# Two transformer blocks on one core: rotation and gates moved into the input projection, chunks run ahead, value products spread

## The reference

```python
def token_mixer(h, w_in, ...):
    proj = h @ w_in
    qk_ml, v_ml, o_ml, gates, q_at, kv_at = jnp.split(proj, cuts, axis=-1)
    qk_ml = jax.nn.silu(causal_dwconv(qk_ml, ml_conv_w, ml_conv_b))
    ...
    i_pre = gates[..., :ML_H] + ml_i_b
    logf = jax.nn.log_sigmoid(gates[..., ML_H:] + ml_f_b)
    h_ml = mlstm_chunkwise(q_ml, k_ml, v_ml, i_pre, logf)
    h_ml = rms_norm(h_ml, ml_norm_g) * jax.nn.sigmoid(o_ml)
    q_at, k_at = rope(q_at, pos), rope(k_at, pos)
    o_at = rms_norm(sliding_window_attention(q_at, k_at, v_at, attn_sinks), attn_norm_g)
    return jnp.concatenate([h_ml, o_at], axis=-1) @ w_out

# mlstm_chunkwise, one chunk (m_t is the running maximum, b the cumulated logf)
sqk = einsum('bhtd,bhsd->bhts', qc, kc) * exp(dmat - m_t[..., None])
num = einsum('bhts,bhsd->bhtd', sqk, vc) + w_inter[..., None] * einsum('bhvk,bhtk->bhtv', C, qc)
den = sum(sqk, -1) + w_inter * einsum('bhk,bhtk->bht', n, qc)
h = num / maximum(abs(den), exp(-m_t))[..., None]
C_new = decay[..., None, None] * C + einsum('bhsv,bhsk->bhvk', vc * ws[..., None], kc)
```

## Time and profile before

| | us |
|---|---|
| median of the runs (2887.23 to 2889.32) | 2887.88 |
| profiled execution | 2889.09 |
| its span, from first to last instruction | 2887.3 |
| TensorE busy | 2528.2 (88%) |
| VectorE busy | 1344.2 (47%) |
| ScalarE busy | 866.9 (30%) |
| mean granted TensorE clock | 0.936 of full |

### The profile page before, as it was taken

One profiled execution on the slowest core, in us unless ns is written; L12 is line 12 of the kernel. 1 busy time (PEld: TensorE's weight loads), 2 busy tenths in 40 slices (PEclk: granted clock), 3 DMA queues, 4 the chain that ended last, 5 costly groups with the idle time before them and its releaser, 6 DMA issues. The chain is left out here.

```text
span 2887.3 us, 29375 instructions
## 1 busy us (share of the span) xinstructions
PE 2528.2 (88%) x11143; PEld 2026.2 (70%) x11143; DVE 1344.2 (47%) x1509; ACT 866.9 (30%) x1185; POOL 283.4 (10%) x212
## 2 busy tenths in 40 slices
PE   4899867365979999999999895888889999999998
PEld 2688666253857888888887582666668888888887
DVE  3554256565255455444445515888452333323333
ACT  2321223165343222222223324777332111111111
POOL 0000000044100000000001230545110000000000
PEclk8899966677989999999999897999899999999999
DMA  6246200200221111111112210000211111111111
GB/s 211 86 139 221 75 0 0 88 0 0 102 88 37 51 44 58 44 51 44 45 50 102 84 52 15 1 0 0 88 44 44 44 49 52 44 51 48 47 51 66
DMA packets 163843, 167.09 MB, mean 58 GB/s; under 512 B 7025, under 2 KB 147137, under 8 KB 162753
## 3 DMA queue, kind: packets, MB, share of 16 engines
q1 hardware_dynamic: 162337, 160.95, 17.2%
q0 software_dynamic: 1440, 5.24, 0.4%
HBM read 144.16 MB, written 22.02 MB: 58 GB/s over the span
## 5 line engine op out<-in xcount | busy, mean ns | idle before, releaser
L263 PE MATMUL ps<-hhi,whi 128*128 128x512 f32 x1984 | 773.5, 390 | 8.2 <-DVE cbuf L779 4.0
L265 PE MATMUL ps<-hhi,wlo 128*128 128x512 f32 x1984 | 772.6, 389 | 0.0
L264 PE MATMUL ps<-hlo,whi 128*128 128x512 f32 x1984 | 772.4, 389 | 0.0
L212 DVE TENSOR_TENSOR wlo<-raw,whi 128x1024 fp32r<-128x1024 f32 x180 | 234.7, 1307 | 523.8 <-ACT whi L207 523.8
L263 PEld LDWEIGHTS ps<-hhi,whi 128*128 128x128 f32 x1984 | 372.9, 188 | 87.6 <-DVE cbuf L779 4.4
L264 PEld LDWEIGHTS ps<-hlo,whi 128*128 128x128 f32 x1984 | 372.9, 188 | 77.4
L265 PEld LDWEIGHTS ps<-hhi,wlo 128*128 128x128 f32 x1984 | 372.7, 188 | 77.4
L207 ACT ACTIVATE whi<-raw 128x1024 fp32r<-128x1024 f32 x180 | 186.4, 1050 | 426.8 <-PE ps L1781 299.9
L1898 DVE TENSOR_TENSOR arena<-arena,ps 128x1024 f32<-128x1024 f32 x176 | 214.8, 1220 | 155.6 <-PE ps L1781 154.5
L1779 PE MATMUL ps<-hid_hi,whi 128*128 128x512 f32 x704 | 275.2, 391 | 0.0
L1780 PE MATMUL ps<-hid_lo,whi 128*128 128x512 f32 x704 | 274.1, 389 | 0.0
(11 more groups left out here) (276 smaller groups left out, 2889.4 us busy)
## 6 DMA issues: line engine op xcount, KB each, us to landing
raw<-in_w_up SPq DMA_DIRECT2D x66, 512.0 KB, 3.7
raw<-in_w_down SPq DMA_DIRECT2D x44, 512.0 KB, 3.4
raw<-in_w_in SPq DMA_DIRECT2D x32, 512.0 KB, 5.5
arena<-in_w_ada SPq DMA_DIRECT2D x32, 512.0 KB, 4.5
x_park<-arena SPq DMA_DIRECT2D x3, 4096.0 KB, 12.5
raw<-in_w_gate SPq DMA_DIRECT2D x22, 512.0 KB, 3.6
cbuf<-in_w_ada SPq DMA_DIRECT2D x16, 512.0 KB, 5.3
raw<-in_w_out SPq DMA_DIRECT2D x16, 512.0 KB, 4.0
```

Source lines behind the costliest of these rows:

```text
L212: nc.vector.tensor_tensor(wlo[:, w.off % RING, :], raw[:, w.off % RAW, :], whi[:, w.off % RING, :].bitcast(F32), ALU.subtract).then_inc(lo ...
L263: nc.tensor.matmul(acc[:, tok], whi[:, s, ws], hhi[:, k, tok], start=(k == 0), stop=False)
L264: nc.tensor.matmul(acc[:, tok], whi[:, s, ws], hlo[:, k, tok], start=False, stop=False)
L265: mm = nc.tensor.matmul(acc[:, tok], wlo[:, s, ws], hhi[:, k, tok], start=False, stop=(k == DK - 1))
```

## The change

In the input projection the tiles get another order: six attention tiles first, then 8 convolution tiles, 4 values, 4 output gates. The gate products come directly behind the pair of the first two tiles. TensorE makes the rotation of tile `ROPED[n]` behind the product of tile n + 2, VectorE does its three operations there, and GpSimd stores the rotated tile. The gate rows are worked out by VectorE and ScalarE in tiles 1 to 5, and three of them are stored in DRAM (`gate_rows`). Blocks `ml_gates` and `rope` are gone. The chunks read keys, queries and values in place, get their three rows by broadcast loads, have two buffers for most things, and turn up to two chunks ahead; the loops over chunks are unrolled. In the second attention the sixteen value matmuls are made in four parts, one in each unit of the next group, into two halves of the accumulator.

```diff
-                return columns(a["w_in"], w + (-T_IN), 8 if o - T_IN >= 16 else 0)
+                r = o - T_IN
+                return columns(a["w_in"], w + (20 if r < 2 else 14 if r < 6 else -6), 8 if r < 6 else 0)
...
+        ROPED = (0, 2, 3, 4, 5)
...
+            @block.sync
+            def _(sp):
+                norm_mix.sp(sp)
+                sp.dma_start(cos_1, a["rope"][:, 0, :]).then_inc(tables_in, 16)
+                sp.dma_start(sin_1, a["rope"][:, 1, :]).then_inc(tables_in, 16)
+                for t in range(4, N_IN + 4):
+                    load(sp, At(t), tile_source(At(t)))
+                    for n in late_at(t - 2):
+                        if n == 0:
+                            sp.wait_ge(rope_step, 3 * len(ROPED))
...
+                norm_mix.pe_pair(pe, 0)
+
+                pe.wait_ge(gate_hi, 2)
...
+                def rotate(n):
+                    t = ROPED[n]
+                    pe.wait_ge(raw_copied, t + 1)
+                    if n:
+                        pe.wait_ge(rope_step, 3 * n - 2)
+                    for hf in range(2):
+                        tok = slice(hf * HALF, (hf + 1) * HALF)
+                        mm = nc.tensor.matmul(down[0][:, tok], rotA[:, :], cbuf[:, t % 4, tok], start=True, stop=True)
+                    mm.then_inc(rotated, 1)
+
+                for t in range(2, N_IN):
+                    pe.wait_ge(up_free, t + 1)
+                    product(pe, up[t % 2], At(t))
+                    if 2 <= t <= 6:
+                        rotate(t - 2)
...
+                    if t == 2:
+                        act.wait_ge(g_dve, 4)
+                        nc.scalar.activation(row_a, row_a, ACT.Exp, scale=-1.0).then_inc(g_act, 1)
...
+                def rope(r):
+                    t = ROPED[r]
+                    c = cbuf[:, t % 4, :]
...
+                    dve.wait_ge(rotated, r + 1)
+                    nc.vector.tensor_tensor(turned_sin, down[0][:, :], sin_1, ALU.mult).then_inc(rope_step, 1)
+                    nc.vector.tensor_tensor(c, c, cos_1, ALU.mult).then_inc(rope_step, 1)
+                    dve.wait_ge(rope_step, 3 * r + 2)
+                    nc.vector.tensor_tensor(c, c, turned_sin, ALU.add).then_inc(rope_step, 1)
...
+                for t in range(18, N_IN):
+                    pool.wait_ge(up_free, t + 3)
+                    pool.dma_start(spill[:, t - 18, :], cbuf[:, t % 4, :]).then_inc(spilled[t % 4], 16)
+                pool.wait_ge(rows_stored, 48)
+                for i in range(4):
+                    pool.wait_ge(spilled[i], 16 * (3 if i < 2 else 2))
...
+        with nc.Block("ml_chunks") as block:
...
+                for c in range(NB):
+                    if c >= 2:
+                        sp.wait_ge(c_done, c - 1)
+                    for r, v in enumerate((bc_a, bc_w, bc_m)):
+                        sp.dma_start(v[c % 2], rows_dram[r][:, tok(c)].partition_broadcast(P)).then_inc(rows_in[c % 2], 16)
+                sp.wait_ge(c_turned, NB)
+                sp.dma_start(kvq, spill[:, 4:10, :]).then_inc(kvq_in, 16)
...
+                turn(0)
+                update(0)
+                turn(1)
+                for c in range(NB):
+                    outputs(c)
+                    if c + 2 < NB:
+                        turn(c + 2)
+                    if c + 1 < NB:
+                        update(c + 1)
...
+                def exponents(c):
+                    dve.wait_ge(rows_in[c % 2], 48 * (c // 2 + 1))
+                    if c >= 2:
+                        dve.wait_ge(c_main, c - 1)
+                    nc.vector.tensor_tensor(weights_[c % 2], bc_a[c % 2],
+                                            causal[:, :].unsqueeze(1).to_broadcast([P, ML_H, P]), ALU.add).then_inc(c_arg, 1)
...
+                for c in range(NB):
+                    if c + 1 < NB:
+                        weigh(c + 1)
...
+                    dve.wait_ge(c_den, 3 * c + 3)
+                    dve.wait_ge(c_read, c + 1)
+                    nc.vector.tensor_tensor(hml[:, :, tok(c)], hml[:, :, tok(c)], m, ALU.mult).then_inc(c_done, 1)
+                    if c + 2 < NB:
+                        exponents(c + 2)
...
-            ps_t, ps_o = down[0], down[1][:, 0:512]
+            ps_t = down[0]
+            ps_o = [down[1][:, 0:512], down[1][:, 512:1024] if full else down[1][:, 0:512]]
...
-                            if gr_before(n, e) is not None:
-                                values(gr_before(n, e), ((e - 1) // units) % 2, unit(n, e) + (-1))
+                            if group_under(n, e) is not None:
+                                if full:
+                                    part = e % units
+                                    values(group_under(n, e), 1 - e // units, unit(n, e) + (-1),
+                                           range(2 * part, 2 * part + 2))
...
-        rope_stage("rope", 0, rotA, True, False)
         attention("attn", False, Heads())
```

More of the change, by code:

```diff
@@ L8 @@
+import math
 from contextlib import ExitStack
@@ L696, in block_kernel @@
         qk, vt = ar(0, DK, T), ar(32, ML_H, T)
[L697 to L721, removed]
+        hml = qk[:, 0:ML_H, :]
+        cos_1, sin_1, turned_sin = ar(48, T), ar(52, T), ar(56, T)
         late_row = [ar(48 + 4 * i, D) for i in range(3)]
@@ L745, in late_add @@
[L745 to L823, removed]
@@ new lines, in block_kernel @@
+        value_tok = [heads(ar(68, 512)), heads(gateF[:, :, :].rearrange("p a b -> p (a b)"))]
+        state = heads(cbuf[:, 3, :], 2 * P)
+        ps_num, ps_den, ps_s = heads(up[0][:, 0:512]), up[1][:, 0:512], heads(up[1][:, 512:1024])
+        ps_k, ps_v, ps_u = heads(down[0][:, 0:512]), heads(down[0][:, 512:1024]), down[1]
+        qa = ar(16, 4, T)
+        ka, va = ar(32, T), ar(36, T)
+        kvq = ar(16, 6, T)
+        rows_in = [sem("chunk_rows0"), sem("chunk_rows1")]
+        c_turned, c_tokens, c_arg, c_exp, c_query, c_weights, c_ones = (
+            sem("chunk_" + x) for x in ("turned", "tokens", "exponents", "exps", "queries", "weights", "decays"))
@@ new lines, in block_kernel, with tok, _ @@
+        c_main, c_update, c_read, c_den, c_den_free, c_state, c_zero, c_done, kvq_in = (
+            sem("chunk_" + x) for x in ("outputs", "update", "read", "den", "den_free", "state", "zero", "done", "kvq"))
+        with nc.Block("ml_chunks") as block:
+            def tok(c):
+                return slice(c * P, (c + 1) * P)
+            @block.sync
+            def _(sp):
+                for c in range(NB):
[5 more added lines that the diff above has]
+                sp.dma_start(kvq, spill[:, 4:10, :]).then_inc(kvq_in, 16)
+                sp.wait_ge(kvq_in, 16)
@@ L995, in body @@
-                    for h in range(ML_H):
-                        mm = nc.tensor.matmul(ps_u[:, h * 256:h * 256 + 256], ktok[:, h, :], vw[:, h, :], start=True,
-                                              stop=True)
-                    mm.then_inc(c_upd, 1)
-                    if more:
-                        early(c + 1)
-                        pe.wait_ge(c_den, c.val(2, 2))
-                        pe.wait_ge(c_read, c.val(add=1))
-                        late(c + 1)
-                chunk_loop(pe, ahead, body)
+                    mm.then_inc(c_main, 1)
```

490 lines of the change are left out of this document (304 added, 186 removed).

## The result

The changed kernel takes 2850.14 us (median; 2847.13 to 2854.65) against 2888.6 for the kernel before beside it (2887.23 to 2890.31): a ratio of 0.987, 95% interval 0.9858 to 0.9883. It is faster by 38 us (1.3%) where I had forecast 89, and lies outside my range of 2783 to 2840. The profiled execution took 2854.65 us.

The account below looks back on a forecast made before the run. TensorE was taken to bound the input projection, serial chains the gate, rope and chunk stages, VectorE the second attention. Savings 13.9 + 19.5 + 35.4 + 21 = 89.8 from 2889.1 gave 2799 us, range 2783 to 2840.

Parts of the forecast that it names:

- L: Chunks: time of the three broadcast loads, taken as 5.0 us, exposed on VectorE in chunks 2 to 7 and once at the start.
- Rival A: Chunks: the three broadcast loads don't overlap, each taking 3 to 3.7 us, about 10 together; time 2836; chance 0.20.
- Rival D: Chunks: all reads of one array go through one place in memory; at 20 us a load, time 2904; chance 0.03.
- The estimate of 3.8 us: Chunks: broadcast load time from a fixed 2.0 us plus bytes at 436 GB/s; sum some 8 us lower; not adopted.
- The sum around L: Chunks: start, six periods and end give 127.2 us against 146.7, 19.5 saved; 7 us lost per us more of load.
- the periods: Chunks: six periods of 15.15 us each, made of load, mask to weights, weights, state and scaling.
- the start: Chunks: from block start to the first state update, 20 us (17 to 24).
- the end: Chunks: after state 6 the last outputs end 9 us later, then the last chunk takes 7.3 us.
- Input projection: Gate products moved behind the first pair, rotations added on TensorE; chunks start at 357.3 instead of 371.2, saving 13.9 us.
- Rope stage: Stage before the chunks, dropped whole with the 3 MB reload hidden; 35.4 us saved.
- Second attention: Value matmuls in four parts; a block takes 26.2 us against 29.18, seven blocks save 21 us.
- Rival B: Second attention: parts stand in series with the turn; block 28.2 us, only 7 us saved, time 2813; chance 0.12.

## Why the prediction was wrong

**The step that failed is the size of L**, the time of a chunk's three broadcast loads: taken as 5.0 us, it is 12.3. I had bounded it by 3.5 and 12.6 and taken the value near the slope of larger loads, "nearest to the load of the same run length". That load has another address for each partition. Own addresses gave 4.7, so for such loads the slope was right; what it could not tell was that 128 partitions reading one piece, with all pieces a multiple of 4096 bytes apart, move a quarter as fast. Rival A was right that the loads don't overlap, and too low in price (10, or 10.3 by the 5.3 in its sum). Rival D, reads that meet in one place of the memory, is nearest to what the layouts showed; it had 3 in 100 and was priced only from 17.8 up, so 12.3 fell between the rivals. The estimate of 3.8 us that I made from the Trainium skill (DMA: Bandwidth & Descriptors, Anatomy of one DMA) rests on a fit for DMAs that GpSimd issues; SyncE issues these, and the wait was 12.3. My range reached 2840 and thus left out the upper bound of L that I had myself worked out: 12.6 gives 2799 + 7 x 7.6 = 2852.

**The sum around L held.** "7 us lost for each us more of L" gives 2799 + 7 x 7.3 = 2850 with the measured L, and 2850.14 was measured. That this agrees to 0.2 us is luck: the profiled execution took 2854.65, and the smaller errors below partly cancel. With L at 4.7, the kernel with own addresses took 2797.4. Period minus wait is 9.8 us there (14.5 - 4.7), 9.8 in the changed kernel (22.1 - 12.3) and 9.7 without a wait; I had 10.15. The wait after `c_done` exposes the load wholly, as argued: taking it away removed all of it. The chunks took 179.9 us where I had 127.2: the periods are 6 x 7.0 of that, the start 9 (first state update after 29.3 us instead of 20), the end 1.5.

**Input projection: right.** 13.1 us saved against 13.9. TensorE had no gap up to its last product, which ends at 352.2 (352.4 predicted); the copy, the store at 353.61 and its 2.9 us follow, and the blocks change at 358.1, 1.6 after the landing where I had 0.5.

**Rope stage: right, with a price unseen.** The stage is gone. The 3 MB reload is over before it is needed, but it is issued 0.5 us behind the last chunk's rows and runs beside them: that wait is 13.39 instead of 12.1, and with pieces at 4224 bytes it was 11.58 instead of 6.6. Where the rows load fast it hardly shows (4.92 instead of 4.6 with own addresses). That the reload causes it is read from the times of issue, not tested.

**Second attention: right in kind, 2.8 us too low** (23.8 against 21). Blocks of 25.8 at the full clock are below the 26.2 that I had; where the clock is 0.94 they take 27.3. Rival B (28.2) is out, and with it the fear that the parts stand in series.

**What I had left out:** the stages between lost 5.5 us in the profiled execution. 2.8 of them lie in the long feed-forward part from the norm on (its 769.3 us became 772.1), where TensorE's clock came up at another time after its waits (0.85 and 0.91 between 851.6 and 881 us, where the same stretch before had 1.00). The kernels with own addresses and with a place for each chunk had 770.7 and 769.2 there, so this isn't the change's doing but moves from kernel to kernel. The net is 89.8 - 52.7 - 0.8 + 2.8 - 5.5 + 0.6 (the first attention's start, 11.8 instead of 12.4) = 34.2, and 34.5 was the difference of the spans.

## What to carry over

A double buffer whose next load waits for the last reader of the same buffer hides nothing when that reader runs just ahead of the first user: look at what frees a buffer, not at how many there are, and give loads of data that is ready long before a place of their own. Where the trace has no load of the kind that a change adds, the price belongs near the bounds and the range must hold both of them, the more so when one unknown is multiplied by seven. When all partitions read the same few hundred bytes, store them so that what is read together is one run; twelve neighbouring pieces did as well, and padding by one whole piece nearly so.

## What the hardware showed

- Shared reads in pieces of 512 bytes, all a multiple of 4096 bytes apart, moved 80 to 90 GB/s in one load and no more over three DMAs; the same bytes moved 340 to 350 GB/s as twelve neighbouring pieces, up to 479 as runs of 6 KB, and up to 334 from own addresses.
- 512 bytes of padding a row were worth 56 us of this kernel (2850 to 2794), 128 bytes only 32.
- In the chunks the granted clock was 0.68 at a period of 22.1 us, 0.81 at 14.5 and 0.92 at 9.7, with the same matmuls a chunk: the work came closer together and the clock with it.
